# Output projections of a two-layer encoder step: six or five of eight weight blocks loaded before the stage, the first tile taken in two column halves, part of the preparation on GpSimd

## What is computed

```python
mixed = concat(attention outputs) * silu(g)          # 1024 columns, 16 heads x 64
x = x + gate(c) * (mixed @ w_out)
# after layer 1 also: x = rms_norm(x, final_norm_g)
```

## Time and profile before

| | us |
|---|---|
| runs, median of 3 | 1790.69 |
| runs, lowest and highest | 1790.61, 1797.92 |
| the profiled execution's own time | 1794.25 |
| span in the profile, first to last instruction | 1792.4 |
| PE busy in the span | 1644.7 (92%) |
| DVE, ACT, POOL busy | 1260.8, 806.8, 226.9 |

### The profile page before, as it was taken

One profiled execution on the slowest core, in us unless ns is written; L12 is line 12 of the kernel. 1 busy time (PEld: TensorE's weight loads), 2 busy tenths in 40 slices (PEclk: granted clock), 3 DMA queues, 4 the chain that ended last, 5 costly groups with the idle time before them and its releaser, 6 DMA issues. The chain is left out here.

```text
span 1792.4 us, 34047 instructions
## 1 busy us (share of the span) xinstructions
PE 1644.7 (92%) x12751; PEld 1298.2 (72%) x12822; DVE 1260.8 (70%) x2750; ACT 806.8 (45%) x1777; POOL 226.9 (13%) x314
## 2 busy tenths in 40 slices
PE   4688999999999969989997998998996999999798
PEld 1576577777888847767776877787884777787687
DVE  2577577779989938778887645636545888888764
ACT  3457322211112128768884226512215777877321
POOL 2222000000000022101000000010005322330000
PEclk7799999999999979999998998999997999999899
DMA  9314156643243149999845734323425111111632
GB/s 320 81 40 110 62 142 200 206 147 136 61 136 118 47 128 240 231 229 215 222 139 167 261 141 128 109 82 108 102 64 110 30 29 39 48 30 46 199 120 93
DMA packets 212243, 229.26 MB, mean 128 GB/s; under 512 B 122265, under 2 KB 146433, under 8 KB 211058
## 3 DMA queue, kind: packets, MB, share of 16 engines
q1 hardware_dynamic: 205202, 207.17, 41.4%
q0 software_dynamic: 6880, 19.92, 2.9%
HBM read 169.72 MB, written 54.16 MB: 125 GB/s over the span
## 5 line engine op out<-in xcount | busy, mean ns | idle before, releaser
L905 PE MATMUL PS<-ab_wh,hT 128*128 128x512 f32 x576 | 231.9, 403 | 3.8 <-DVE ab_wl L1256 3.8
L906 PE MATMUL PS<-ab_wl,hT 128*128 128x512 f32 x576 | 226.3, 393 | 0.0
L907 PE MATMUL PS<-ab_wh,hT 128*128 128x512 f32 x576 | 225.8, 392 | 0.0
L1449 DVE TENSOR_SCALAR_CACHE_REDUCE topk_junk<-scores,topk_small 128x528 bf16<-128x528 f32 (+6 forms) x224 | 194.6, 915 | 1.3
L1214 ACT ACTIVATE ab_nat<-PS 128x512 f32<-128x512 f32 x54 | 32.2, 597 | 230.7 <-PE PS L907 230.6
L2666 DVE CUSTOM_DVE_ANT_0 la_S<-PS,la_mask 128x128 f32<-128x128 f32 (+4 forms) x144 | 107.5, 746 | 40.6 <-PE PS L907 36.6
L905 PEld LDWEIGHTS PS<-ab_wh,hT 128*128 128x128 f32 x576 | 108.8, 189 | 31.6 <-issue 5.8
L907 PEld LDWEIGHTS PS<-ab_wh,hT 128*128 128x128 f32 x576 | 108.6, 189 | 24.9
L906 PEld LDWEIGHTS PS<-ab_wl,hT 128*128 128x128 f32 x576 | 108.8, 189 | 21.6
L905 PE MATMUL PS<-out_wh,out_mT 128*128 128x512 f32 x288 | 115.8, 402 | 4.7 <-DVE out_mT L2111 4.7
L1808 ACT ACTIVATE at_P<-at_S,at_nm 128x128 f32<-128x128 f32 (+2 forms) x144 | 110.5, 768 | 17.0 <-DVE at_nm L1853 16.7
(11 more groups left out here) (427 smaller groups left out, 4264.1 us busy)
## 6 DMA issues: line engine op xcount, KB each, us to landing
ab_wl_raw<-in_ab_w_in SPq DMA_DIRECT2D x64, 256.0 KB, 5.2
spare<-in_ada_w SPq DMA_DIRECT2D x32, 512.0 KB, 4.0
out_g<-scratch_gates_nat SPq DMA_DIRECT2D x18, 512.0 KB, 5.8
at_vc<-in_cache_a_v SPq DMA_DIRECT2D x8, 1024.0 KB, 10.0
at_vc<-in_cache_b_v SPq DMA_DIRECT2D x8, 1024.0 KB, 5.5
scratch_qcT<-c_T SPq DMA_DIRECT2D x72, 96.0 KB, 2.0
mod_ada_w<-in_ada_w SPq DMA_DIRECT2D x6, 1024.0 KB, 10.3
c_wl_raw<-in_c_w_in SPq DMA_DIRECT2D x24, 256.0 KB, 6.2
```

What stands on the lines that cost most here:

```text
L905: nc.tensor.matmul(out, x[0], w[0], start=start, stop=False)
L906: nc.tensor.matmul(out, x[0], w[1], start=False, stop=False)
L907: return nc.tensor.matmul(out, x[1], w[0], start=False, stop=stop)
L1449: go(V.tensor_scalar(mark, x, limit, 0.0, op, ALU.add, accum_out=cnt[:, m:m + 1]), 0 if m == M - 1 else 1)
```

## The change

In each output stage:

- Weight blocks 2 to 5 (layer 0) or 2 to 4 (layer 1) are also loaded during the attention, over tensors that the attention no longer needs: in layer 0 over slots 1 and 2 of the keys (after head 14 is scored) and over `at_kc1` (after the last cached keys are turned), in layer 1 over slot 0 of `la_k` (after head 13 is scored) and over `la_xs` (after GpSimd's last expansion). SP issues them at the end of the attention's list, after the gates of tile 0. In the output stage SP issues the gates of tile 1 first, then the remaining blocks.
- Tile 0 is divided, gated, turned, rounded and multiplied in two halves of 512 columns (heads 0 to 7 and 8 to 15). DVE takes the first half, GpSimd the division and gating of the second. The sums are inverted in three parts: those of tile 0, of tile 1, and of tiles 2 to 7.
- The remainders of weight blocks 3, 5 and 7 are taken by GpSimd, the other five by DVE.
- On DVE `gate_rows(2)` comes before `low(1)` instead of behind it. On ACT the first rounding of the tile comes after two weight blocks instead of three.
- After the attention of layer 0, 18 further semaphores, of the projection before it and of the opening, are cleared and freed at the barrier. `gated`, `tr_done` and the counters of `mT` count from tile 1.

```diff
-def retire_semaphores(nc):
-
-    nc.clear_and_free_semaphores(list(IN_USE))
+def retire_semaphores(nc, stores=()):
+
+    nc.clear_and_free_semaphores(list(IN_USE) + [STORES.pop(n) for n in stores])
     IN_USE.clear()
     nc.all_engine_barrier()
...
+def shared_spots(nc, stack, name, shape, dt, later, n):
+
+    with nc.sbuf_tensor(name, shape, dt) as tensor:
+        pass
+    raw, low = overlaid(nc, stack, later, [P, n, D])
+    return tensor, raw, low
+
...
-        q, k, decay = sb("q", [P, 3, SEQ], BF16), sb("k", [P, 3, 2, SEQ], BF16), out.raw
+        q, k0, decay = sb("q", [P, 3, SEQ], BF16), sb("k0", [P, 2, SEQ], BF16), out.raw
+        k = [k0, c.at_k[:, 0], c.at_k[:, 1]]
...
-        kc, vc, vn = [c.spare, sb("kc1", [P, nk, HD])], sb("vc", [P, 2, nk, HD]), sb("vn", [TS, 2, HD])
+        kc, vc, vn = [c.spare, c.at_kc1], sb("vc", [P, 2, nk, HD]), sb("vn", [TS, 2, HD])
...
-            out.fetch_weights(sp)
+            out.fetch_weights(sp, range(2))
             sp.wait_ge(built, 6)
             out.fetch_gates(sp)
+            sp.wait_ge(scored, head_at(G - 2, QT - 1) + 1)
+            out.fetch_weights(sp, range(2, 4))
+            sp.wait_ge(turned, number["keys", G - 1, NP - 1] + 1)
+            out.fetch_weights(sp, range(4, 6))
 
...
-        self.w_in, self.g_in = [S("w_in0"), S("w_in1")], S("g_in0")
+        self.w_in, self.g_in = [S(f"w_in{k}") for k in range(2 + len(spots))], S("g_in0")
...
-    def fetch_weights(self, sp):
-        for k in range(2):
-            sp.dma_start(self.raw[:, k, :], self.w_dram[k * P:(k + 1) * P, :]).then_inc(self.w_in[k], 16)
+        self.spots = [self.raw[:, k, :] for k in range(2)] + [raw for raw, low in spots]
+        self.parts = [self.w[:, k, :] for k in range(2)] + [low for raw, low in spots]
+
+    def fetch_weights(self, sp, ks):
+        for k in ks:
+            sp.dma_start(self.spots[k], self.w_dram[k * P:(k + 1) * P, :]).then_inc(self.w_in[k], 16)
 
...
-                    sp.wait_ge(gated, i - 1)
+                    if i == 2:
+                        for part in part_gated:
+                            sp.wait_ge(part, 1)
+                    else:
+                        sp.wait_ge(gated, i - 2)
...
-            for k in range(2, KT):
+            load_gates(1)
+            for k in range(READY, KT):
                 sp.dma_start(raw(k), out.w_dram[k * P:(k + 1) * P, :]).then_inc(w_in[k], 16)
-                if k == 3:
-                    load_gates(1)
             load_x(0)
...
+        ON_POOL = (3, 5, 7)
+        on_vector = [k for k in range(KT) if k not in ON_POOL]
+
+        @block.gpsimd
+        def _(pool):
+            pool.wait_ge(first_inverted, 1)
+            mv = c.mix[:, 0, HALVES[1]].rearrange("p (h d) -> p h d", d=DH)
+            nc.gpsimd.tensor_tensor(mv, mv, rinv[:, 0, HC // 2:].unsqueeze(2).broadcast_to([P, HC // 2, DH]), ALU.mult).then_inc(rows_scaled, 1)
+            pool.wait_ge(rows_scaled, 1)
+            pool.wait_ge(g_in[0], 16)
+            nc.gpsimd.tensor_tensor(c.mix[:, 0, HALVES[1]], c.mix[:, 0, HALVES[1]], g(0)[:, HALVES[1]], ALU.mult).then_inc(part_gated[1], 1)
+            for k in ON_POOL:
+                pool.wait_ge(w_hi, k + 1)
+                nc.gpsimd.tensor_tensor(wl(k), raw(k), wh[:, k, :], ALU.subtract).then_inc(pool_lo, 1)
+
...
+            def turn_part(a):
+                pe.wait_ge(part_gated[a], 1)
+                for k in range(4 * a, 4 * a + 4):
+                    last = nc.tensor.transpose(PS[:, a, (k % 4) * P:(k % 4 + 1) * P], c.mix[:, 0, k * P:(k + 1) * P], c.ident[:])
+                last.then_inc(part_turned, 1)
+
+            for a in range(2):
+                turn_part(a)
             for k in range(KT):
-                pe.wait_ge(w_lo, k + 1)
+                pe.wait_ge(part_lo, k // 4 + 1)
+                if k in ON_POOL:
+                    pe.wait_ge(pool_lo, ON_POOL.index(k) + 1)
+                else:
+                    pe.wait_ge(w_lo, on_vector.index(k) + 1)
...
-            for k in range(3):
+            for k in range(2):
                 split_high(k)
-            high(0)
-            for k in range(3, KT):
+            for a in range(2):
+                act.wait_ge(part_turned, a + 1)
+                nc.scalar.activation(mT[:, 0, 0, 4 * a:4 * a + 4].rearrange("p a b -> p (a b)"), PS[:, a, :], ACT.Copy).then_inc(part_hi, 1)
+                split_high(2 + a)
+            for k in range(4, KT):
                 split_high(k)
...
+                if k in ON_POOL:
+                    return
...
+            def low_part(a):
+                dve.wait_ge(part_hi, a + 1)
+                nc.vector.tensor_tensor(mT[:, 0, 1, 4 * a:4 * a + 4].rearrange("p a b -> p (a b)"), PS[:, a, :],
+                                        mT[:, 0, 0, 4 * a:4 * a + 4].rearrange("p a b -> p (a b)"), ALU.subtract).then_inc(part_lo, 1)
+
+            nc.vector.reciprocal(rinv[:, 0, :], c.sums[:, 0, :]).then_inc(first_inverted, 1)
+            dve.wait_ge(first_inverted, 1)
+            mv = c.mix[:, 0, HALVES[0]].rearrange("p (h d) -> p h d", d=DH)
+            chain(nc.vector.tensor_tensor(mv, mv, rinv[:, 0, 0:HC // 2].unsqueeze(2).broadcast_to([P, HC // 2, DH]), ALU.mult))
+            dve.wait_ge(g_in[0], 16)
+            nc.vector.tensor_tensor(c.mix[:, 0, HALVES[0]], c.mix[:, 0, HALVES[0]], g(0)[:, HALVES[0]], ALU.mult).then_inc(part_gated[0], 1)
+            split_low(0)
+            low_part(0)
+            split_low(1)
+            split_low(2)
+            low_part(1)
+            split_low(3)
+            chain(nc.vector.reciprocal(rinv[:, 1, :], c.sums[:, 1, :]))
             gate_rows(1)
+            chain(nc.vector.reciprocal(rinv[:, 2:, :], c.sums[:, 2:, :]))
             for k in range(4, KT):
                 split_low(k)
+            gate_rows(2)
             low(1)
-            gate_rows(2)
...
-            out.fetch_weights(sp)
+            out.fetch_weights(sp, range(2))
             sp.wait_ge(spread, 1)
             out.fetch_gates(sp)
+            sp.wait_ge(scored, head_at(HC - 3, QT - 1) + 1)
+            out.fetch_weights(sp, range(2, 4))
+            sp.wait_ge(expanded, wide_ops(len(wide) - 1))
+            out.fetch_weights(sp, range(4, 5))
...
-            out = OutLoads(nc, c, 0, ins["ab_w_out"][0], inner)
+            c.at_k, raw, low = shared_spots(nc, inner, "at_k", [P, 2, 2, SEQ], BF16, "out0_wl23", 2)
+            c.at_kc1, raw2, low2 = shared_spots(nc, inner, "at_kc1", [P, PAST // P, HD], F32, "out0_wl45", 2)
+            spots = [(a[:, n, :], b[:, n, :]) for a, b in ((raw, low), (raw2, low2)) for n in range(2)]
+            out = OutLoads(nc, c, 0, ins["ab_w_out"][0], inner, spots)
             branches_ab(nc, c, out)
-            retire_semaphores(nc)
+            retire_semaphores(nc, [n for n in STORES if n.split("_")[0] in ("ix", "ab", "cum", "first")])
...
-            out = OutLoads(nc, c, 1, ins["c_w_out"][0], inner)
+            with nc.sbuf_tensor("la_k", [P, 2, 2, 2, SEQ], BF16) as c.la_k:
+                pass
+            raw, low = overlaid(nc, inner, "out1_wl23", [P, 2, D])
+            inner.enter_context(nc.sbuf_tensor("la_k1", [P, 2, 2, SEQ], BF16))
+            c.la_xs, raw2, low2 = shared_spots(nc, inner, "la_xs", [P, 2, 512], F32, "out1_wl4", 1)
+            spots = [(a[:, n, :], b[:, n, :]) for a, b, m in ((raw, low, 2), (raw2, low2, 1)) for n in range(m)]
```

More of the change, by code:

```diff
@@ L63 @@
 STORE_NAMES = [f"{p}_nat_out{n}" for p in ("ix", "ab", "c") for n in range(4)] + ["cum_out", "first_keys"] + [
-    f"out{l}_{m}{n}" for l in range(2) for n in range(2) for m in ("stored", "row")] + ["out0_w_in0", "out0_w_in1", "out0_g_in0"] + [
+    f"out{l}_{m}{n}" for l in range(2) for n in range(2) for m in ("stored", "row")] + [f"out0_w_in{k}" for k in range(6)] + ["out0_g_in0"] + [
     f"ab_w_in{k}" for k in range(KT)]
@@ L1702, in score_head @@
                     for d in range(2):
-                        last = nc.tensor.matmul(PS[:, to + a // 512, 0:w], q[:, g % 3, i * P:(i + 1) * P], k[:, g % 3, d, a:a + w],
+                        last = nc.tensor.matmul(PS[:, to + a // 512, 0:w], q[:, g % 3, i * P:(i + 1) * P], k[g % 3][:, d, a:a + w],
                                                 start=d == 0, stop=d == 1 and not masked_end)
@@ L1909, in mixed_out @@
     S = lambda n: semaphore(nc, f"out{l}_{n}")
-    w_in, w_hi, w_lo = out.w_in + [S(f"w_in{k}") for k in range(2, KT)], S("w_hi"), S("w_lo")
+    READY = len(out.spots)
+    w_in, w_hi, w_lo = out.w_in + [S(f"w_in{k}") for k in range(READY, KT)], S("w_hi"), S("w_lo")
     g_in, x_in = [out.g_in, S("g_in1")], [S("x_in0"), S("x_in1")]
@@ L1913, in mixed_out @@
     half_done, mm_done, y_read, y_done, link, std_done, sq_done = S("half"), S("mm"), S("y_read"), S("y"), S("link"), S("std"), S("sq")
```

(21 more changed lines are left out.)

23 lines of the change are left out of this document (11 added, 12 removed).

## The result

| | before | after |
|---|---|---|
| median of the runs beside one another, us | 1791.83 (20 runs) | 1798.63 (20 runs) |
| ratio, with its 95% interval | | 1.0032 [1.0022, 1.0042] |
| the profiled execution's own time | 1794.25 | 1795.67 |
| span | 1792.4 | 1793.6 |
| PE, DVE, POOL busy | 1644.7, 1260.8, 226.9 | 1642.3, 1264.9, 254.0 |

The change costs 0.3% (0.0032 of 1791.8 is 5.7 us, by the interval 3.9 to 7.5). The loss is within the 0.5% taken as no change, but the median lies 1.6 us above the range (1.1 of that is the kernel before itself, 1791.83 in twenty runs and 1790.69 in the three that the forecast was added to), and the mechanism is that of the slower rival.

The account below looks back on a forecast made before the run. PE, busy 92% of the span, bounds the kernel; only the output stages' openings could change. Layer 0 loses 0.4, layer 1 gains 1.0, barrier costs 0.2: 1794.25 less 0.4 gives 1793.9 us, median 1790.3; range 1775.5 to 1797.

Parts of the forecast that it names:

- the slower rival: Output stages, division of tile 1 to block 6: GpSimd holds DVE its whole duration; loss 4.0 to 7.0 us; chance 0.12.
- Loads, order, barrier: Output stages: early loads cost nothing, layer 1's tile 2 gates at 17.1 us, PE waits of 2.03 and 2.79 go; barrier 0.2.
- The first tile: Opening of each output stage: first product at 5.4 us instead of 7.9, GpSimd holding DVE 0.9 us per half operation.
- the held time of a remainder: Output stages: each weight remainder on GpSimd, 2.2 us long, holds DVE off for 1.8 us.
- The clock term: Behind PE's 3.6 us wait for block 4 the clock halves: 0.2 us per product, some 1.2 us.
- The sum: Tile 1 at 25.6 us: layer 0 loses 0.4, layer 1 gains 1.0, barrier costs 0.2; a gain of 0.4 us.
- No contention: Output stages: DVE and GpSimd run side by side; gain 13.1 us, to 1777.6; chance 0.32.

Follow-up runs that it names:

- The filled wait: The changed kernel with 16 matmuls that nobody needs put before PE's wait for block 4 in both output stages; 1791.75 us, ratio 1.0000 to the kernel before.

## Why the prediction missed

- **Loads, order, barrier.** Right: ACT waits for no weight block, and there is no wait of PE for the gating of tile 2. Wrong: the gates of tile 2 in layer 1, forecast at about 17.1, land at about 20.4 (1684.24 less 1663.88, with nothing on GpSimd), so nine loads at 1.9 us each was too little. The changed kernel hides that: DVE comes to them at 19.8 without a wait in the first trace and waits 0.59 us in the second. The forecast of tile 1 at 19.7 without contention rested on the 17.1. Barrier: 0.41 measured, 0.2 taken, inside the bounds.
- **The first tile.** In layer 1 the first product came at 5.3 against the 5.4 forecast, in layer 0 at 6.2. There GpSimd began 0.06 us ahead of DVE's division (952.88 and 952.94), so DVE was held twice, 0.84 and 0.94 us; I had given DVE the first turn. The 0.9 taken for a half operation was right in size.
- **The step that failed is the held time of a remainder**, "0.9 us per 1024 elements of one tensor", so 1.8 of 2.2 us. It was scaled by the number of tensors from a pair of the opening in which GpSimd worked on one tensor with a scalar. That pair's 0.90 was read rightly, the scalar form in the output stage shows it again, but it doesn't carry over: beside a remainder DVE waits for nearly all of it (2.07 us waited in the pair of one remainder, 2.1 held of 2.2). Block 4 was forecast near 16.7 us and came at 18.5 and 17.6. In layer 1 the 0.9 are three holds of 0.3 more; in layer 0 the first tile adds 0.8.
- **The clock term was mis-sized**: 1.2 us taken, 2.4 measured in layer 0 (5.23 against 2.83) and 2.2 in layer 1 (5.02 less 2.82). At 0.2 us a product 1.2 us is six products; all 12 of blocks 4 and 5 were slow in layer 0 and nearly all in layer 1. The filled wait shows this term alone.
- **The sum.** Tile 1 was forecast at 25.6 in both: 2.5 too early in layer 0 and 1.4 in layer 1, with 0.2 for the barrier 4.1 us, which leads from the forecast gain of 0.4 to the loss of 3.7 that the trace shows. Of the 4.1 the holds of the remainders are about 1.9, the first tile 0.8, the clock 2.2 and the barrier 0.2; the steps behind block 4 otherwise took 0.9 less than forecast. So the hold alone would not have made this loss: the clock is as large a part.
- **The rivals.** The slower rival named the place, the mechanism and the price: tile 1 at 27.8 and a loss of 4.0, up to 7.0 with the clock. It had 0.12. Of the Trainium skill's rule in "SBUF — State Buffer", section "Who interferes with whom", that the second of two such operations waits for the whole of the first, the trace agrees for two-tensor work on both engines: 2.07 us of 2.20. For the scalar form it doesn't agree: 0.9 us of 2.85, in the opening and in the output stage. I held the opening's 0.90 against the rule, a row of another form.
- "No contention" is refuted by the pairs above. Its gain of 13.1 us, 0.9927, was not reached without GpSimd either: 0.9950, with tile 1 at 20.9 and 22.8 and not at 18.8 and 19.7, as DVE does the remainders itself there and the gates of tile 2 are late in layer 1.

## What to carry to other kernels

Before work is moved from VectorE to GpSimd, look at what VectorE does at that time: if both read two tensors from SBUF they take turns, whole operation by whole operation, and moving a 1.22 us operation costs VectorE up to 2.2 us. Such work belongs into stretches where VectorE reads PSUM or one tensor: in the changed kernel the low part at 960.85 (0.68 us) and the reciprocal at 961.45 (0.24) lost nothing beside a remainder. No run here moved the work there. And price the wait that a delay makes on TensorE with the clock behind it: here, with one remainder moved, 2.1 us of delay became 4.8 in layer 0.
